# Two transformer blocks on one core: the down projections with products of 512 columns

## The chip, the cores and the metric

One core of a Trainium2 chip runs the whole program in one launch. The metric is device time in microseconds, from the first to the last instruction of the program, as the median of several runs.

## The reference

Two stacks of two layers each follow one another over 256 positions of width 1024, in float32. All four layers end in a feed-forward part with 2816 hidden units, and its last step is the down projection that this case is about:

```
first stack:   y = (silu(g) * v) @ w_out        (g, v: halves of a width-3 causal convolution of h @ w_in)
second stack:  y = (silu(x @ w_gate) * (x @ w_up)) @ w_down
both:          x = x + gate * rms_norm(y) * gain  (no gate in the second stack)
```

Ahead of the feed-forward parts stand a convolution mixer and differential attention (first stack), an RWKV-7 time mix and a gating unit with a spatial product (second stack). The first stack also takes shifts, scales and gates from `silu(c) @ mod_w`, a product of a vector with a 1024 x 12288 matrix, called the modulation below.

## The kernel before

Activations lie transposed: channels on the 128 partitions, the 256 positions along the free axis (`T = 256`), in 8 chunks of channels (`DC`) or 22 chunks of hidden units (`FC`). A float32 product is made of rounded operands: a weight tile is split into `hi` (rounded, by ScalarE, `weights_hi`, line 1370) and `lo = raw - hi` (by VectorE, `weights_lo`, line 1919), an operand into a high and a low part too, and the product is lo x high + hi x low + hi x high, three matmuls into one accumulating half bank (lines 740 to 742 in `layer` of the tensor block).

The weights come in units. A unit of a down projection holds 11 tiles of 128 x 128 (1408 columns, 704 KB); two units (even and odd) make one chunk of 128 outputs, over the 22 hidden chunks. So a down stage has 16 units, 8 pairs, and each pair sums 66 products in one bank (PS[0] or PS[2] in turn, columns 0 to 255). There are four such stages: ffn0_down, ffn1_down, glu0_down, glu1_down. Every other stage has units of 8 tiles (1024 columns). Units go through four slots of `raw`, `hi` and `lo`, and each engine goes through the units in order, in bodies of four units:

- SyncE issues the load of a unit's raw weights when `lo` of the unit four before is made, then the loads of the modulation rows that ride there.
- ScalarE, at unit u: rounds the weights of unit u + 2 (when TensorE is done with unit u - 2), then, at an odd unit, waits for TensorE's unit u and evacuates the bank (`with_square`): Square into `SQ` (line 1426), then Copy with a gain into `Y` (line 1427), which frees the bank.
- VectorE, at unit u: `lo` of unit u + 2, then the evacuation of its own, which the down stages don't have, then the riders: `mod_unit` (line 1925) multiplies 1024 modulation weights by the condition and sums them. ffn0_down has riders of 2, 1, 2 and 0 after the four units of every body; the other three down stages have none. After the last unit of ffn0_down, glu0_down and others the low parts of the next stage's first units are made in the same places.
- TensorE, at unit u: waits for `lo` of unit u and for the bank to be free, then makes the products.

The hidden units are split by GpSimd into `GH` and `GL` (line 2738 and 2740). Behind a down stage `out_layer` sums the squares over the channels with TensorE (line 757; GpSimd adds seven of the eight squares beforehand, line 2729), ScalarE takes the root, VectorE the inverse, TensorE spreads it (line 764), and VectorE's `residual` scales `Y` and adds it to `X` (lines 1978 and 1983). The next stage's operands follow from that. `keep_busy` (line 615) makes filler products with a constant tile.

Of the kernel before, what the change touches and what calls it, by code (L numbers as in the profile page):

```python
# [25 lines left out]
F32R = mybir.dt.float32r  # L26
ALU = mybir.AluOpType
ACT = mybir.ActivationFunctionType
AX_X = mybir.AxisListType.X
ds = bass.ds  # L30

P = 128
D = 1024
T = 256
# [162 lines left out]
def program(nc, w8, w11, wmod, par, con, xin, relb, crow, lora_in, lora_out, sgu_ws, sgu_bs, out):  # L197
    scratch = nc.dram_tensor("rel_bias_rows", (HEADS, 384), F32, kind="Internal").ap()

    with ExitStack() as ctx:  # L200
# [48 lines left out]
        def at(place, name, shape, dt=F32, plus=0):  # L249
            return nc.alloc_sbuf_tensor_at(name, shape, dt, offset=arena + (int(place * F) + plus) // 32 * 32)  # L250
# [6 lines left out]
        tmp = at(4, "tmp", [P, 4, 2, T])  # L257
        GH = at(5, "GH", [P, FC, T], F32R, plus=PHASE)
        GL = at(5, "GL", [P, FC, T], F32R, plus=PHASE + 4 * FC * T)
        modraw = at(5, "modraw", [P, SLOTS, D], plus=PHASE + 8 * FC * T)  # L260
# [350 lines left out]
        def _(pe):  # L611
# [99 lines left out]
            def layer(name, oh, ol, between=None, peel_first=False, fresh=False, after_chunk=None, beside=0, amid=None,  # L711
# [6 lines left out]
                def body(i, last):  # L718
                    both = together and isinstance(i, int) and i == 0
                    if both:  # L720
                        two_units(name, oh, ol, fresh, after_chunk, beside)
                        for r in range(2):
                            if between and start:
                                between(i, r)
                    for r in range(2 if both else 0, SLOTS):
                        u = start + 4 * i + r
                        k0 = kt * (r % 2) if down else 0
                        bank = PS[r - r % 2 if down else r]
                        pe.wait_ge(lo_made, u + 1)
                        if not (fresh and isinstance(i, int) and i == 0):  # L730
                            wait(pe, evac_done, u - 3)
                        elif r == 0:
                            pe.wait_ge(evac_done, start)
                        for k in range(kt):
                            if r == 0 or (down and r == 1):
                                pe.wait_ge(S("hidden_split") if down else operand_ready, ready_at[name] + k0 + k + 1)
                            w = slice(k * P, (k + 1) * P)
                            first = k == 0 and (not down or r % 2 == 0)
                            final = k == kt - 1 and (not down or r % 2 == 1)
                            pe.matmul(bank[:, 0:T], lo[:, r, w], oh[:, k0 + k], start=first, stop=False)  # L740
                            pe.matmul(bank[:, 0:T], hi[:, r, w], ol[:, k0 + k], start=False, stop=False)  # L741
                            ins = pe.matmul(bank[:, 0:T], hi[:, r, w], oh[:, k0 + k], start=False, stop=final)  # L742
                            if amid and k == kt // 2 - 1:
                                amid(i, r)
                            if after_chunk and isinstance(i, int) and i == 0 and r < 3:
                                after_chunk(r, k)
                            if beside and isinstance(i, int) and i == 0 and r == 0 and k < kt - 1:
                                keep_busy(1, 7, beside)
                        ins.then_inc(mm_done, 1)
                        if between:  # L750
                            between(i, r)
# [405 lines left out]
            def first_t(tb):  # L1157

                pe.wait_ge(S("tt_made"), 1)
                pe.wait_ge(S("level_by_act"), tb + 2)  # L1160
# [202 lines left out]
        def _(act):  # L1363
# [44 lines left out]
            def with_square(n, down, gain, biased=False):  # L1408
# [5 lines left out]
                def evacuate(i, r, u):  # L1414
# [3 lines left out]
                    c = 2 * i + r // 2 if down else 4 * i + r  # L1418
                    src = PS[r - 1 if down else r][:, 0:T]
                    if biased:  # L1420
# [369 lines left out]
            for tb in range(2):  # L1790
# [5 lines left out]
                               ).then_inc(S("level_by_act"), 1)  # L1796
            act.wait_ge(S("tt_made"), 1)
            for tb in range(2):
# [111 lines left out]
        def _(dve):  # L1910
# [292 lines left out]
            def conv_ffn_up(name, l):  # L2203
# [16 lines left out]
                layer(name, evacuate, made=1, peel_all=(name != LOOPED))  # L2220

            def glu_up(name, n):
                def evacuate(i, r, u):
# [18 lines left out]
            gate_gain(1, 3 * DC)  # L2242
            layer("ffn0_down", peel_all=True)
            residual(1, par_gain("kv_norm_g", 0))
# [119 lines left out]
            gate_gain(3, 7 * DC)  # L2364
            layer("ffn1_down")
            residual(3)
# [198 lines left out]
            def state_out(k):  # L2565
# [4 lines left out]
                for b in (g, g + 1):  # L2570
# [7 lines left out]
                          ).then_inc(S("tm_made"), 1)  # L2578
            dve.transpose(TTd[:].rearrange("p m t -> p t m"), U[:]).then_inc(S("tt_made"), 1)

# [19 lines left out]
            third_block(1)  # L2600
            dve.wait_ge(S("tt_made"), 1)
            dve.tensor_copy(TT[2 * BLK:3 * BLK, :, 2 * BLK:3 * BLK], TTd[2 * BLK:3 * BLK]).then_inc(S("level_by_dve"), 1)
# [58 lines left out]
            glu_up("glu0_up", 5)  # L2661
            layer("glu0_down", third=True)
            residual(5, par_gain("norm_g2", 4 * DC))
# [53 lines left out]
            glu_up("glu1_up", 7)  # L2717
            layer("glu1_down")
            residual(7)
# [3 lines left out]
        def _(pool):  # L2723
# [6 lines left out]

            flatH, flatL = (x[:].rearrange("p c t -> p (c t)") for x in (GH, GL))

# [131 lines left out]
```

## Time and profile before

| | |
|---|---|
| median of 3 runs | 1419.88 us (1414.57 to 1428.73) |
| the profiled execution, first to last instruction | 1420.2 us |
| granted TensorE clock, mean | 0.996 |
| TensorE busy | 1375.6 us, 97% |
| VectorE busy | 1049.1 us, 74% |
| ScalarE busy | 733.2 us, 52% |
| GpSimd busy | 219.2 us, 15% |

The profiled execution has no other time beside its span. PE is TensorE, PEld its weight loads, DVE is VectorE, ACT is ScalarE, POOL is GpSimd. Matmuls are pipelined and their ends are modelled: one lasts some 280 ns in the rows, while the next begins 113 to 118 ns after it, so their pace is read from starts. A granted clock of 1.00 is 2.4 GHz and one of 0.50 is 1.2 GHz. The four down stages lie at 283 to 345, 622 to 682, 1061 to 1122 and 1349 to 1409 us of the span.

### The profile page before, as it was taken

The numbers are of one execution on the slowest core, as the hardware profiler recorded it, in microseconds if no ns is written. First come the engines' busy times: TensorE is split into PE (matmuls) and PEld (weight loads), VectorE is DVE, ScalarE is ACT, GpSimd is POOL, SyncE is SP. The second block draws the span as 40 slices with busy tenths as digits, with TensorE's granted clock in tenths as the row PEclk, the third lists the DMA queues.
The fourth block names the chain that finished last, engine by engine and source line by source line (L and its number), as shares of the span: only waits on it lengthen the run. The fifth ranks groups of instructions, "written<-read, shape, count | busy, mean of one in ns | idle before, by whom it ended". The sixth has DMA issues, their size and how long they took to land.

```text
span 1420.2 us, 30753 instructions
## 1 busy us (share of the span) xinstructions
PE 1375.6 (97%) x11830; PEld 1310.7 (92%) x11830; DVE 1049.1 (74%) x1649; ACT 733.2 (52%) x1194; POOL 219.2 (15%) x232
## 2 busy tenths in 40 slices
PE   8999999999999999999999999999999999999997
PEld 6998899999988899999878888799999998999997
DVE  7988799987887889974787965777774556677743
ACT  4547555644556556664366442554444447544442
POOL 0000133310000223320000010113320000133300
PEclk9999999999999999999999999999999999999999
DMA  9874367797663547675322300346666433466661
GB/s 377 303 258 171 123 226 234 258 394 252 205 226 105 208 165 254 216 232 173 151 98 90 120 2 2 116 133 186 188 208 203 141 115 120 144 197 197 208 205 69
DMA packets 68434, 258.20 MB, mean 182 GB/s; under 512 B 7545, under 2 KB 9857, under 8 KB 67970
## 3 DMA queue, kind: packets, MB, share of 16 engines
q1 hardware_dynamic: 68354, 257.10, 54.2%
q8 instruction: 54, 0.88, 0.2%
q14 instruction: 26, 0.21, 0.0%
HBM read 256.01 MB, written 1.06 MB: 181 GB/s over the span
## 4 chain that ended last, share of the span: by engine, by line
PE 81%; DVE 11%; ACT 3%; issue 2%; DMA 2%; DVEq 0%; ACTq 0%
PE ps L740 21%; PE ps L742 20%; PE ps L741 20%; PE ps L757 3%; DVE lo L1919 2%; PE ps L701 2%; PE ps L703 1%; PE ps L702 1%; ACT hi L1370 1%; DMA modraw<-in_wmod 1%; DVE U L2508 1%; DMA modlast<-in_wmod 1%; DVE products L2506 1%; DVE modraw L1925 1%; PE ps L764 1%
## 5 line engine op out<-in xcount | busy, mean ns | idle before, releaser
L1919 DVE TENSOR_TENSOR lo<-raw,hi 128x1024 fp32r<-128x1024 f32 (+1 forms) x350 | 476.5, 1378 | 168.5 <-ACT hi L1370 167.8
L740 PE MATMUL ps<-OH,lo 128*128 128x256 f32 x1920 | 540.8, 282 | 6.2 <-DVE lo L1919 6.0
L742 PE MATMUL ps<-OH,hi 128*128 128x256 f32 x1920 | 534.8, 279 | 0.0
L741 PE MATMUL ps<-OL,hi 128*128 128x256 f32 x1920 | 534.8, 279 | 0.0
L1370 ACT ACTIVATE hi<-raw 128x1024 fp32r<-128x1024 f32 (+1 forms) x350 | 381.0, 1112 | 10.4 <-DMA raw<-in_w 6.1
L740 PEld LDWEIGHTS ps<-OH,lo 128*128 128x128 f32 x1920 | 362.0, 189 | 12.7 <-DVE lo L1919 9.9
L741 PEld LDWEIGHTS ps<-OL,hi 128*128 128x128 f32 x1920 | 362.4, 189 | 0.0
L742 PEld LDWEIGHTS ps<-OH,hi 128*128 128x128 f32 x1920 | 361.0, 188 | 0.0
L740 PE MATMUL ps<-GH,lo 128*128 128x256 f32 x704 | 196.3, 279 | 0.0
L742 PE MATMUL ps<-GH,hi 128*128 128x256 f32 x704 | 196.2, 279 | 0.0
L741 PE MATMUL ps<-GL,hi 128*128 128x256 f32 x704 | 196.2, 279 | 0.0
L2738 POOL CAST GH<-tmp 128x256 f32 x88 | 71.0, 807 | 515.5 <-DVE tmp L2201 515.5
L741 PEld LDWEIGHTS ps<-GL,hi 128*128 128x128 f32 x704 | 133.0, 189 | 0.0
L740 PEld LDWEIGHTS ps<-GH,lo 128*128 128x128 f32 x704 | 132.9, 189 | 0.1
L742 PEld LDWEIGHTS ps<-GH,hi 128*128 128x128 f32 x704 | 132.2, 188 | 0.0
L2729 POOL TENSOR_TENSOR SQ<-SQ 128x256 f32<-128x256 f32 x42 | 40.1, 955 | 494.3 <-ACT SQ L1426 494.0
L2740 POOL TENSOR_TENSOR GL<-tmp,GH 128x256 f32 x88 | 98.1, 1115 | 15.3 <-POOL GH L2738 15.3
L1492 ACT ACTIVATE tmp<-ps,par_sb 128x256 f32<-128x256 f32 x88 | 49.5, 565 | 92.8 <-PE ps L742 86.6
L1426 ACT ACTIVATE SQ<-ps 128x256 f32<-128x256 f32 (+1 forms) x56 | 21.5, 384 | 145.5 <-PE ps L742 144.1
L1925 DVE SCALAR_TENSOR_TENSOR modraw<-modraw,cond 128x1024 f32<-128x1024 f32 x71 | 87.0, 1239 | 7.0 <-ACT cond L1513 6.1
L1509 ACT ACTIVATE tmp<-tmp 128x256 f32<-128x256 f32 x44 | 18.4, 418 | 132.2 <-DVE tmp L2231 132.2
L701 PE MATMUL ps<-OH,lo 128*128 128x256 f32 x192 | 61.1, 318 | 10.0 <-DVE OL L2031 3.8
(389 smaller groups left out, 2059.5 us busy)
## 6 DMA issues: line engine op xcount, KB each, us to landing
raw<-in_w SPq DMA_DIRECT2D x288, 512.0 KB, 3.9
raw<-in_w SPq DMA_DIRECT2D x64, 704.0 KB, 5.3
modraw<-in_wmod SPq DMA_DIRECT2D x71, 512.0 KB, 5.2
modlate<-in_wmod SPq DMA_DIRECT2D x10, 512.0 KB, 4.0
modlast<-in_wmod SPq DMA_DIRECT2D x7, 512.0 KB, 4.5
modfirst_a<-in_wmod SPq DMA_DIRECT2D x4, 512.0 KB, 11.4
modfirst_b<-in_wmod SPq DMA_DIRECT2D x4, 512.0 KB, 12.1
l<-in_lora_in SPq DMA_DIRECT2D x1, 1536.0 KB, 6.2
```

The costliest lines, as they stand in the source:

```text
L701: pe.matmul(PS[r][:, 0:T], lo[:, r, w], oh[:, k], start=(k == 0), stop=False)
L740: pe.matmul(bank[:, 0:T], lo[:, r, w], oh[:, k0 + k], start=first, stop=False)
L741: pe.matmul(bank[:, 0:T], hi[:, r, w], ol[:, k0 + k], start=False, stop=False)
L742: ins = pe.matmul(bank[:, 0:T], hi[:, r, w], oh[:, k0 + k], start=False, stop=final)
L757: ins = pe.matmul(PS[4 + h][:, x * P:x * P + SAME], src[:, h * P:(h + 1) * P], ones[:, 0:SAME], start=first, stop=last)
L1370: act.activation(hi[:, s, 0:kt * P], raw[:, s, 0:kt * P], ACT.Copy).then_inc(hi_made, 1)
L1492: act.activation(tmp[:, kind, q], PS[r][:, 0:T], ACT.Identity, scale=flatpar[:, ds(w, 1)], bias=flatpar[:, ds(b, 1)]).then_inc(S("tap2_mad ...
L1919: dve.tensor_tensor(lo[:, s, 0:kt * P], raw[:, s, 0:kt * P], hi[:, s, 0:kt * P].bitcast(F32), ALU.subtract).then_inc(lo_made, 1)
L1925: stt(out=mod_at(m, s), in0=mod_at(m, s), scalar=1.0, in1=cond[:], op0=ALU.mult, op1=ALU.mult, accum_out=mod_sums[:, ds(m, 1)]).then_inc(m ...
L2729: pool.tensor_tensor(SQ[:, 0], SQ[:, 0], SQ[:, c], ALU.add).then_inc(S("sq_added"), 1)
L2738: pool.tensor_copy(flatH[:, ds(2 * T * i + q * T, T)], tmp[:, 3, q]).then_inc(S("hidden_hi"), 1)
L2740: pool.tensor_tensor(flatL[:, ds(2 * T * i + q * T, T)], tmp[:, 3, q], flatH[:, ds(2 * T * i + q * T, T)].bitcast(F32), ALU.subtract).then ...
```

## The change

`GH` and `GL` become the two halves of one tile `GB` at the same addresses. In the down stages the two products with `hi` become one: `hi` against both halves, 2 x 256 columns, into the whole bank. The product with `lo` still goes into the bank's first half. At every odd unit VectorE waits for TensorE and adds the two halves of the bank with a reduce into one of two slots of `xt` in SBUF; ScalarE waits for that and reads `xt` where it read the bank. Apart from that, two semaphores of the time mix become one (`tt_made` joins `tm_made`).

```diff
-        GH = at(5, "GH", [P, FC, T], F32R, plus=PHASE)
-        GL = at(5, "GL", [P, FC, T], F32R, plus=PHASE + 4 * FC * T)
+        GB = at(5, "GB", [P, 2, FC, T], F32R, plus=PHASE)
+        GH, GL = GB[:, 0], GB[:, 1]
...
                             final = k == kt - 1 and (not down or r % 2 == 1)
+                            if down:
+                                if first:
+                                    pe.matmul(bank[:, :], hi[:, r, w], GB[:, :, k0 + k], start=True, stop=False)
+                                    pe.matmul(bank[:, 0:T], lo[:, r, w], oh[:, k0 + k], start=False, stop=False)
+                                else:
+                                    pe.matmul(bank[:, 0:T], lo[:, r, w], oh[:, k0 + k], start=False, stop=False)
+                                    ins = pe.matmul(bank[:, :], hi[:, r, w], GB[:, :, k0 + k], start=False, stop=final)
+                                continue
                             pe.matmul(bank[:, 0:T], lo[:, r, w], oh[:, k0 + k], start=first, stop=False)
...
-                pe.wait_ge(S("tt_made"), 1)
+                pe.wait_ge(S("tm_made"), 2)
...
-                    src = PS[r - 1 if down else r][:, 0:T]
+                    if down:
+                        act.wait_ge(S("halves_added"), c + (DC * (n // 2) + 1))
+                    src = xt[:, 2 + r // 2] if down else PS[r][:, 0:T]
...
+            def add_halves(i, r, u):
+
+                if r % 2:
+                    dve.wait_ge(mm_done, u + 1)
+                    dve.tensor_reduce(xt[:, 2 + r // 2], PS[r - 1][:, :].rearrange("p (h t) -> p t h", h=2), AX_X, ALU.add
+                                      ).then_inc(S("halves_added"), 1)
...
-            layer("ffn0_down", peel_all=True)
+            layer("ffn0_down", add_halves, peel_all=True)
...
-            layer("ffn1_down")
+            layer("ffn1_down", add_halves)
...
-            layer("glu0_down", third=True)
+            layer("glu0_down", add_halves, third=True)
...
-            layer("glu1_down")
+            layer("glu1_down", add_halves)
```

`add_halves` is VectorE's evacuation: it stands behind the low part and ahead of the riders of its unit.

## Rows read from the trace of the kernel before

**Rows 1.** The page, busy time and share of the span by engine.

```profile
PE 1375.6 (97%) x11830; PEld 1310.7 (92%) x11830; DVE 1049.1 (74%) x1649; ACT 733.2 (52%) x1194; POOL 219.2 (15%) x232
```

**Rows 2.** The page, the chain that ended last, by line.

```profile
PE ps L740 21%; PE ps L742 20%; PE ps L741 20%; PE ps L757 3%; DVE lo L1919 2%; PE ps L701 2%; PE ps L703 1%; PE ps L702 1%; ACT hi L1370 1%; DMA modraw<-in_wmod 1%; DVE U L2508 1%; DMA modlast<-in_wmod 1%; DVE products L2506 1%; DVE modraw L1925 1%; PE ps L764 1%
```

**Rows 3.** Stages: window, us; busy (instructions) of PE, PEld, DVE, ACT, POOL; clock; DMA; GB/s.

```profile
282.60:345.00 62.40, 62.40 (x534) 62.32 (x533) 51.75 (x64) 27.30 (x34) 9.10 (x10) 1.00 0.91 348
618.60:680.50 61.90, 61.90 (x549) 61.90 (x548) 30.35 (x26) 29.18 (x36) 8.15 (x10) 1.00 0.57 185
...
1347.00:1409.00 62.00, 62.00 (x549) 62.00 (x548) 26.38 (x19) 25.53 (x31) 5.71 (x9) 1.00 0.42 143
```

**Rows 4.** Groups by line and form: busy us, mean ns, idle before.

```profile
L740 PE MATMUL ps<-GH,lo 128*128 128x256 f32 x704 | 196.3, 279 | 0.0
```

**Rows 5.** Timeline of ACT, three down stages: start, us, line, tiles, idle before.

```profile
290.51 0.38 ACT L1426 ACTIVATE SQ<-ps 128x256 f32 x1 [0.78 <-PE ps L742]
...
298.43 0.38 ACT L1426 ACTIVATE SQ<-ps 128x256 f32 x1 [3.60 <-PE ps L742]
...
306.20 0.39 ACT L1426 ACTIVATE SQ<-ps 128x256 f32 x1 [4.49 <-PE ps L742]
306.48 0.47 ACT L1427 ACTIVATE Y<-ps,rgain 128x256 f32 x1
306.84 1.38 ACT L1370 ACTIVATE hi<-raw 128x1408 fp32r<-128x1408 f32 x1
...
629.65 0.38 ACT L1426 ACTIVATE SQ<-ps 128x256 f32 x1 [1.95 <-PE ps L742]
...
637.12 0.39 ACT L1426 ACTIVATE SQ<-ps 128x256 f32 x1 [4.18 <-PE ps L742]
...
1114.67 0.38 ACT L1426 ACTIVATE SQ<-ps 128x256 f32<-128x256 f32 x1 [4.39 <-PE ps L742]
...
1118.62 1.06 ACT L1370 ACTIVATE hi<-raw 128x1024 fp32r<-128x1024 f32 x1 [1.30 <-PE ps L742]
1122.45 0.38 ACT L1426 ACTIVATE SQ<-ps 128x256 f32<-128x256 f32 x1 [2.77 <-PE ps L742]
```

**Rows 6.** Timeline of PE: products of 288 rounded columns, filler in unrounded float32.

```profile
48.73 0.30 PE L632 MATMUL ps<-dL,utH 128*128 128x288 f32 x1
...
49.27 0.29 PE L633 MATMUL ps<-dH,utH 128*128 128x288 f32 x1
...
694.19 2.11 PE L615 MATMUL ps<-con_sb 128*128 128x256 f32 x9
```

**Rows 7.** Groups by line and form: the reduces out of a bank.

```profile
L2309 DVE TENSOR_REDUCE small<-ps 128x2 f32<-128x512 f32 x8 | 5.5, 689 | 3.4 <-PE ps L892 3.4
...
L2309 DVE TENSOR_REDUCE small<-ps 128x2 f32<-128x256 f32 x8 | 3.3, 412 | 0.0
```

**Rows 8.** The chain that ended last, end of ffn0_down: start, us, what.

```profile
344.81 0.13 PE ps L742
...
344.97 0.39 ACT SQ L1426
...
345.40 0.70 PE ps L757 x4
```

**Rows 9.** Timeline of DVE, ffn0_down.

```profile
292.33 1.62 DVE L1919 TENSOR_TENSOR lo<-raw,hi 128x1408 fp32r<-128x1408 f32 x1
293.86 1.22 DVE L1925 SCALAR_TENSOR_TENSOR modraw<-modraw,cond 128x1024 f32<-128x1024 f32 x1
...
295.01 1.62 DVE L1919 TENSOR_TENSOR lo<-raw,hi 128x1408 fp32r<-128x1408 f32 x1
...
338.92 1.22 DVE L1919 TENSOR_TENSOR lo<-raw,hi 128x1024 fp32r<-128x1024 f32 x1 [0.76 <-ACT hi L1370]
```

**Rows 10.** Stages as in rows 3, around the first drop of the granted clock.

```profile
696.30:698.70 2.40, 0.33 (x3) 0.36 (x4) 2.37 (x6) 0.81 (x2) 0.00 (x0) 1.00 0.00 0
698.80:702.20 3.40, 3.40 (x18) 3.40 (x17) 3.33 (x9) 0.81 (x2) 0.00 (x0) 0.50 0.02 5
```

More of the change, by code:

```diff
@@ L1796, in _ @@
                                ).then_inc(S("level_by_act"), 1)
-            act.wait_ge(S("tt_made"), 1)
+            act.wait_ge(S("tm_made"), 2)
             for tb in range(2):
@@ L2578, in _ @@
                           ).then_inc(S("tm_made"), 1)
-            dve.transpose(TTd[:].rearrange("p m t -> p t m"), U[:]).then_inc(S("tt_made"), 1)
+            dve.transpose(TTd[:].rearrange("p m t -> p t m"), U[:]).then_inc(S("tm_made"), 1)
             def level_copy(to, bank, rows, width):
@@ L2600, in _ @@
             third_block(1)
-            dve.wait_ge(S("tt_made"), 1)
+            dve.wait_ge(S("tm_made"), 2)
             dve.tensor_copy(TT[2 * BLK:3 * BLK, :, 2 * BLK:3 * BLK], TTd[2 * BLK:3 * BLK]).then_inc(S("level_by_dve"), 1)
@@ L2729, in add_up @@
                     pool.tensor_tensor(SQ[:, 0], SQ[:, 0], SQ[:, c], ALU.add).then_inc(S("sq_added"), 1)
-            flatH, flatL = (x[:].rearrange("p c t -> p (c t)") for x in (GH, GL))
+            flatH, flatL = (x.rearrange("p c t -> p (c t)") for x in (GH, GL))
             def split_hidden(k):
```

## The prediction

> **What bounds the kernel now.** I read the busy line of the page first: TensorE is busy for 97% of the span and VectorE for 74% [rows 1]. The chain that ended last says whether that is the limit: 61% of it are the three products of line 740 to 742 [rows 2]. So a product saved is time saved, as long as nothing else becomes late. The four down stages then show what the average hides [rows 3]: TensorE is full in all four, but VectorE is busy for 51.75 of 62.40 us in ffn0_down and for 30.35 us of ffn1_down and 26.38 us of glu1_down (glu0_down lies between). The difference is the modulation: only ffn0_down carries riders (2, 1, 2 and 0 of them after the four units of a body).
>
> **The products.** Before, each of the 704 pairs of a weight tile and an operand chunk makes three products of 256 columns, so there are three groups like the one shown [rows 4]. After, it makes one of 256 and one of 512: as many columns, 704 weight loads and 704 instructions fewer. What is gained is only what a product costs beyond its columns. The pace before comes from ScalarE's Square, which runs once per pair of units, that is per 66 products: 306.20 - 298.43 = 7.77 us in ffn0_down and 1122.45 - 1114.67 = 7.78 us in glu0_down, but 637.12 - 629.65 = 7.47 us in ffn1_down, and glu1_down goes like it [rows 5]. So one product takes 0.118 us in two stages and 0.1133 us in the other two. Both paces occur in the same code at the same granted clock (1.00 [rows 3]), and each holds until the next stall; I assume that a stage keeps its pace.
>
> No rounded product of 512 columns stands in the trace. From below: nine filler products of unrounded float32 run back to back in 2.11 us [rows 6]. If the last one's record outlasts the next start as the 288-column records do (0.30 - 0.135 = 0.165 us), each takes (2.11 - 0.165) / 9 = 0.216 us, the longest streamed product that the trace has. From above: two products at the present pace, 0.2266 or 0.236. The widest rounded products, those of 288 columns, follow each other at (49.27 - 48.73) / 4 = 0.135 us [rows 6], so 0.017 us for 32 more columns against 0.118; by that slope, 512 would take 0.254, the far end. I take 0.220, between 0.216 and twice the better pace and nearer to the first, since a longer product leaves its successor's weight load more time to hide. At 0.1133 a pair then goes from 0.3400 to 0.3333 us, 6.7 ns x 176 = 1.2 us per stage; at 0.118 from 0.354 to 0.338, 16 ns x 176 = 2.8 us. For ffn1_down, glu0_down and glu1_down together that is 1.2 + 2.8 + 1.2 = 5.2 us less. ffn0_down is counted apart, below.
>
> The Trainium skill (TensorE: Matmul & The Clock Gate, section Back-to-back issue gap) gives an isolated gap of N / 2.4 + 2.5 ns, which is 216 ns for 512 columns and 109 ns for 256. The trace has 113 to 118 for 256, so the rule leaves out something here; with its 216 in place of 220 the three stages would gain another 2 us.
>
> **The adds at the end of a stage.** Each of the four stages makes eight sums on VectorE, 32 in all, each of 512 inputs to 256 outputs out of a bank. The nearest row is the same operation with as many inputs out of a bank, 0.689 us; with half as many it takes 0.412, my lower end [rows 7]. That the two halves lie 256 elements apart has no row; twice the first, 1.38 us, is my upper end. I take 0.69. In the middle of a stage the sum lies beside TensorE's next pair of units in the other bank (7.4 us for 0.69 and ScalarE's 0.7). Behind the last pair nothing covers it: the chain there goes from the last product to the Square, to the token sums, to the root [rows 8], and the sum with one hand-over of 0.03 us stands in front of the Square. That is 0.72 us in each of ffn1_down, glu0_down and glu1_down: 2.2 us more. ScalarE's Square and scaling read SBUF in place of a bank; I count that as nothing. The two semaphores made one, and the two tiles made one at the same addresses, cost nothing.
>
> **ffn0_down: a new ring.** Here the sum also adds a wait, and that is the largest term. VectorE works in order. At an odd unit it will make the low part that it makes now, then wait for the product and add, then do its rider. ScalarE, in order too, now waits for the sum, does Square and scaling, and only then rounds the next weight tile, which VectorE needs for its next low part. So one sum starts the chain that leads to the next sum. Its period, from rows of this stage: the sum 0.69, hand-over 0.03, Square 0.28 and scaling 0.36 to the next start, the rounding 1.38, hand-over 0.03 [rows 5]: 2.77 us until the low part can start (a rider of 1.15 fits into this time, and the rest of it VectorE idles); the low part 1.53 and two riders of 1.15, each to the next start, and the second low part 1.53 [rows 9]. Together 8.13 us, against 7.4 to 7.8 us in which TensorE does a pair. Behind this ring wait TensorE (for the low part) and, at the end, the residual.
>
> It also starts late. In the trace VectorE is free of the low part of unit 3 at 293.86, though the first bank is full at 290.4 (the Square of it starts at 290.51) [rows 5, 9]. The first sum thus starts at 293.86, 3.4 us late. Six periods follow, and a last one with tiles of 1024 columns (rounding 1.06, low parts 1.22 less 0.09 [rows 5, 9]): 2.45 + 1.13 + 2.30 + 1.13 = 7.01. The last sum starts at 293.86 + 6 x 8.13 + 7.01 = 349.7, and the last Square at 350.4, where it stands at 344.97 now [rows 8]: 5.4 us later. TensorE itself gets the low part of unit 4 at 293.86 + 2.77 + 1.62 = 298.2, that of unit 14 five periods later at 338.9, and ends two units (7.4 us) on, at 346.3: whatever its products gain in this stage is lost to waiting, and it then idles for 4 us.
>
> In the other three stages there are no riders, and the same ring takes 2.77 + 1.53 + 1.53 = 5.83 us, less than a pair's 7.3: no wait there.
>
> Twice in the trace the granted clock is 0.50, that is 1.2 GHz, for 3.4 us, and both times TensorE had been idle just before; the place shown is that near 700 us, with products in only 0.33 of 2.40 us before it [rows 10], the other lies near 1194. So I expect the same after the 4 us in ffn0_down. The work in these 3.4 us (token sums, spreading, filler, the first products of att_k) mostly waits for VectorE. Bounds: nothing, or half of 3.4 us; I take 0.9.
>
> **The sum**, against the profiled span of 1420.2 us (the median of the runs is 1419.88, so the profile stands for it): - 5.2 + 2.2 + 5.4 + 0.9 = + 3.3, so 1423.5 us, 0.2% slower. A measurement of this kernel tells about 1% from no change: the three runs spread from 1414.57 to 1428.73.
>
> **Rivals.**
> - The ring does not form: the sums fall into VectorE's 10.65 idle us of ffn0_down (eight need 5.5), and all four stages gain. 1420.2 - 5.2 - 2.8 + 4 x 0.72 = 1415.1. For it: the idle time is there. Against: it lies before low parts, waiting for ScalarE's rounding [rows 9], and the ring makes just that wait longer.
> - A strided sum out of a bank is dear. Each 0.1 us more counts eleven times (eight in the ring, three ends). At 1.38 us: 1431. From 1.65 us on the kernel is over 1% slower (1434.1). For it: no row has this stride. Against: both reduce forms of the trace go by the number of inputs (0.689 for 512, 0.412 for 256 [rows 7]).
> - 512 columns cost two products of the stage's pace: no gain, 1428.7. For it: the 288-column rows scale even more steeply than the columns. Against: the unrounded products show that a longer one closes the gap.
> - A 512-column product is far cheaper than its columns. At 0.131 us a pair of units would need 22 x (0.1133 + 0.131) = 5.4 us, the ring's 5.83 us would bind in the three stages, each would end 12 to 13 us sooner, and the time would be 1386. The 288-column row, already at 0.135, speaks against it. The same section of the Trainium skill states 131 ns for a sustained stream of N = 512 with its weight loads; no run here shows such a stream.
>
> **How the numbers follow.** Forecast 0.60, no ring 0.13, dear sum 0.12, no gain 0.12, cheap product 0.01, and 0.02 for what I don't see. Unknown prices around the forecast: the sum at 0.42 gives - 3.0 and at 1.38 + 7.6; the product at 0.216 gives - 2.1, at 0.236 + 8.4 and at 0.254 + 18; the clock - 0.9 to + 0.8. The pace that a stage falls into (0.0045 us per product, 4.8 us for an up stage of 1056) can differ from run to run by several us either way. From the low sides together and the run spread I take 1412, from the likelier high ones 1437. Over 1% faster (under 1406) holds only the cheap product and luck: 0.02. Over 1% slower takes the dearest sum, or the dear sum and no gain together: 0.08.
>
> **What would show it.** Right: 704 products of 512 columns, 0.21 to 0.23 us from start to start; a group of 32 sums near 0.69 us; in ffn0_down Squares 8.1 us apart, VectorE's low parts idle for ScalarE before the even units, the last Square about 4 us after the last product, and granted clock 0.5 soon after; in the other three stages Squares 7.3 to 7.5 us apart and a last Square 0.7 us after the last product. Wrong: sums much over 0.7 us, Squares in ffn0_down at 7.4 us, or a 512-column product that takes as long as two.

## The result, and the profile after

| | before | after |
|---|---|---|
| median, runs taken in turn | 1427.16 us (20 runs, 1414.55 to 1436.38) | 1435.12 us (20 runs, 1429.56 to 1440.78) |
| ratio of the times | | 1.0078, interval 1.0054 to 1.0101 |
| the profiled execution, its span | 1420.2 us | 1432.8 us |
| granted TensorE clock, mean | 0.996 | 0.993 |

By the ratio the change makes the kernel 0.8% slower; the two medians by themselves stand 8.0 us or 0.6% apart, which lies just inside the interval. The forecast was 0.2% slower, 1423.5 us; the sign and the mechanism in ffn0_down came as forecast, and one term was wrong in sign.

The page's busy time by engine, after [rows 1]:

```profile
PE 1382.7 (97%) x11126; PEld 1285.0 (90%) x11126; DVE 1071.0 (75%) x1681; ACT 735.1 (51%) x1194; POOL 216.4 (15%) x232
```

704 matmuls fewer, and TensorE is busy 7 us longer. VectorE's extra 22 us are the sums. The groups by line and form, after (busy us, mean ns, idle before); 32 more pairs of products stand under other lines of the same block [rows 4, 7]:

```profile
L746 PE MATMUL ps<-GB,hi 128*128 128x512 f32 x672 | 238.5, 397 | 0.0
L745 PE MATMUL ps<-GB,lo 128*128 128x256 f32 x672 | 188.7, 281 | 0.0
L2236 DVE TENSOR_REDUCE xt<-ps 128x256 f32<-128x512 f32 x32 | 22.0, 689 | 42.8 <-PE ps L746 42.8
```

The sum takes 0.689 us, the same as the reduce of as many inputs before [rows 7]. The stages after, with the columns of [rows 3]: ffn0_down, ffn1_down, glu1_down, and the second clock level behind ffn0_down:

```profile
282.90:345.30 62.40, 60.86 (x339) 51.85 (x338) 50.44 (x63) 25.70 (x32) 6.54 (x9) 1.00 0.89 333
628.80:691.20 62.40, 62.40 (x358) 54.27 (x356) 32.22 (x29) 27.69 (x33) 5.56 (x8) 1.00 0.53 172
1359.00:1421.00 62.00, 62.00 (x355) 53.95 (x354) 28.79 (x25) 25.33 (x30) 5.57 (x8) 1.00 0.43 140
353.50:357.00 3.50, 3.50 (x11) 2.93 (x12) 2.43 (x7) 2.86 (x5) 0.00 (x0) 0.51 1.04 345
```

ffn0_down is no longer full of products: TensorE is busy for 60.86 of 62.40 us in it. ffn1_down and glu1_down are full, but a full stage now takes longer. From the first product to the last, the four down stages took 62.0, 59.7, 62.1 and 59.7 us before and take 64.9, 61.8, 61.8 and 61.8 us after: the two that had the better pace have lost it. Where the time was lost along the program is read from the first scaling of each residual behind a down stage. VectorE's timeline, before and then after:

```profile
347.39 0.75 DVE L1978 TENSOR_TENSOR Y<-Y,ps 128x256 f32<-128x256 f32 x2 [0.80 <-PE ps L764]
...
684.40 1.28 DVE L1978 TENSOR_TENSOR Y<-Y,ps 128x512 f32<-128x512 f32 x2 [0.87 <-PE ps L764]
...
1124.87 0.75 DVE L1978 TENSOR_TENSOR Y<-Y,ps 128x256 f32<-128x256 f32 x2 [0.80 <-PE ps L764]
...
1412.05 1.28 DVE L1978 TENSOR_TENSOR Y<-Y,ps 128x512 f32<-128x512 f32 x2 [0.87 <-PE ps L764]
```

```profile
354.57 0.75 DVE L1988 TENSOR_TENSOR Y<-Y,ps 128x256 f32<-128x256 f32 x2 [1.21 <-PE ps L772]
...
694.51 1.29 DVE L1988 TENSOR_TENSOR Y<-Y,ps 128x512 f32<-128x512 f32 x2 [0.87 <-PE ps L772]
...
1134.38 0.75 DVE L1988 TENSOR_TENSOR Y<-Y,ps 128x256 f32<-128x256 f32 x2 [0.80 <-PE ps L772]
...
1424.66 1.28 DVE L1988 TENSOR_TENSOR Y<-Y,ps 128x512 f32<-128x512 f32 x2 [0.87 <-PE ps L772]
```

After is 7.2 us late behind ffn0_down, 10.1 behind ffn1_down, 9.5 behind glu0_down and 12.6 behind glu1_down. So the loss is in ffn0_down (7.2) and in ffn1_down and glu1_down (about 3 each); glu0_down costs 0.7. Between ffn1_down and glu0_down 1.3 us come back, 0.7 of them in the time mix, in this one execution.

**The ring in ffn0_down.** ScalarE's timeline after: two Squares and what stands between them, the last Square of the stage, and two Squares of ffn1_down [rows 5, 8]:

```profile
303.06 0.42 ACT L1436 ACTIVATE SQ<-xt 128x256 f32 x1 [4.95 <-DVE xt L2236]
303.39 0.49 ACT L1437 ACTIVATE Y<-xt,rgain 128x256 f32 x1
303.79 2.63 ACT L1378 ACTIVATE hi<-raw 128x1408 fp32r<-128x1408 f32 x2
...
311.38 0.42 ACT L1436 ACTIVATE SQ<-xt 128x256 f32 x1 [4.96 <-DVE xt L2236]
...
351.71 0.42 ACT L1436 ACTIVATE SQ<-xt 128x256 f32<-128x256 f32 x1 [4.43 <-DVE xt L2236]
...
637.71 0.42 ACT L1436 ACTIVATE SQ<-xt 128x256 f32 x1 [2.95 <-DVE xt L2236]
...
645.48 0.42 ACT L1436 ACTIVATE SQ<-xt 128x256 f32 x1 [4.40 <-DVE xt L2236]
```

The Squares in ffn0_down are 8.32 us apart (7.77 before), and each waits for the sum. In ffn1_down they are 7.77 apart (7.47 before); there TensorE is never idle, so that is the pace of the products. VectorE's timeline gives the start of the sum ahead of the first of these Squares:

```profile
302.25 0.68 DVE L2236 TENSOR_REDUCE xt<-ps 128x256 f32<-128x512 f32 x1
```

The chain that ended last shows what VectorE does in front of the last sum of ffn0_down:

```profile
346.37 1.23 DVE lo L1929
347.59 2.29 DVE modraw L1935 x4
349.88 1.14 DVE lo L1929
351.01 0.61 DVE xt L2236
...
351.71 0.43 ACT SQ L1436
...
690.93 0.24 PE ps L746
...
691.20 0.70 DVE xt L2236
...
691.99 0.43 ACT SQ L1436
```

At the end of ffn0_down the sum comes behind a low part, two riders and another low part; at the end of ffn1_down it comes straight behind the last product, and there the Square starts 1.06 us after the start of that product; before it was 0.16 [rows 8]. Of the 0.90 more the product is 0.11 longer (0.24 for 0.13), and the sum with its hand-overs is 0.8. TensorE's timeline after, behind ffn0_down:

```profile
347.79 0.39 PE L746 MATMUL ps<-GB,hi 128*128 128x512 f32 x1
...
352.18 0.69 PE L765 MATMUL ps<-con_sb,SQ 128*128 128x96 f32 x4 [3.57 <-ACT SQ L1436]
...
353.42 1.12 PE L772 MATMUL ps<-con_sb,tok 128*128 128x128 f32 x4
354.33 3.63 PE L615 MATMUL ps<-con_sb 128*128 128x256 f32 x10
```

The last Square is 3.9 us behind the start of the last product, TensorE idles for 3.57 us, and from 353.5 to 357.0 the granted clock is 0.51, near 1.2 GHz (windows above).

### The profile page after: what moved, and what is told of

Same layout as the page of the kernel before. It is cut to its first block, busy times and chain, and to the rows that moved or that the text cites. A ratio compares the mean times of both kernels' runs of the same rounds, so it can differ in the third digit from the quotient of the medians.

```text
span 1432.8 us, 29418 instructions
## 1 busy us (share of the span) xinstructions
PE 1382.7 (97%) x11126; PEld 1285.0 (90%) x11126; DVE 1071.0 (75%) x1681; ACT 735.1 (51%) x1194; POOL 216.4 (15%) x232
## 3 DMA queue, kind: packets, MB, share of 16 engines
HBM read 256.01 MB, written 1.06 MB: 179 GB/s over the span
## 4 chain that ended last, share of the span: by engine, by line
PE 78%; DVE 15%; ACT 4%; issue 2%; DMA 1%; ACTq 0%; DVEq 0%
PE ps L748 15%; PE ps L750 14%; PE ps L749 14%; PE ps L746 9%; PE ps L745 4%; DVE lo L1929 4%; PE ps L765 3%; DVE modraw L1935 2%; PE ps L701 2%; ACT hi L1378 2%; PE ps L702 1%; PE ps L703 1%; DMA modraw<-in_wmod 1%; PE ps L615 1%; DVE U L2525 1%
## 5 line engine op out<-in xcount | busy, mean ns | idle before, releaser
L746 PE MATMUL ps<-GB,hi 128*128 128x512 f32 x672 | 238.5, 397 | 0.0
L745 PE MATMUL ps<-GB,lo 128*128 128x256 f32 x672 | 188.7, 281 | 0.0
L746 PEld LDWEIGHTS ps<-GB,hi 128*128 128x128 f32 x672 | 126.3, 188 | 29.2
L2755 POOL CAST GB<-tmp 128x256 f32 x88 | 71.0, 807 | 513.9 <-DVE tmp L2211 513.9
L745 PEld LDWEIGHTS ps<-GB,lo 128*128 128x128 f32 x672 | 126.1, 188 | 1.5
L2757 POOL TENSOR_TENSOR GB<-tmp,GB 128x256 f32 x88 | 98.2, 1116 | 16.5 <-POOL GB L2755 16.5
L1436 ACT ACTIVATE SQ<-xt 128x256 f32 (+1 forms) x32 | 13.4, 418 | 143.5 <-DVE xt L2236 138.6
L615 PE MATMUL ps<-con_sb 128*128 128x256 f32 (+1 forms) x262 | 67.4, 395 | 2.3 <-ACT Btok L1786 1.2
L615 PEld LDWEIGHTS ps<-con_sb 128*128 128x128 f32 x262 | 49.9, 204 | 11.0 <-DMA con_sb<-in_con 2.0
```

Source lines behind the costliest of these rows:

```text
L615: pe.matmul(PS[bank][:, 0:width], ones, con_sb[:, 0:width], start=True, stop=True)
L745: pe.matmul(bank[:, 0:T], lo[:, r, w], oh[:, k0 + k], start=False, stop=False)
L746: ins = pe.matmul(bank[:, :], hi[:, r, w], GB[:, :, k0 + k], start=False, stop=final)
L2755: pool.tensor_copy(flatH[:, ds(2 * T * i + q * T, T)], tmp[:, 3, q]).then_inc(S("hidden_hi"), 1)
L2757: pool.tensor_tensor(flatL[:, ds(2 * T * i + q * T, T)], tmp[:, 3, q], flatH[:, ds(2 * T * i + q * T, T)].bitcast(F32), ALU.subtract).then ...
```

## The experiments

Two theories of the loss stood after this. The first: 512 rounded columns cost two products of the worse pace, in any surroundings, and the ring and the last sums cost the rest. The rival: the sums, the waits or the alternation of widths slow the products, and a 512-column product alone is cheaper. Beside it stood the question of the two paces.

### The product by itself

```diff
+            row(N, 0, lambda r, w, c: mm(T, hi[:, r, w], GB[:, 0, c]))
+            row(N, 0, lambda r, w, c: mm(2 * T, hi[:, r, w], GB[:, :, c]))
...
+            row(N, 0, lambda r, w, c: mm(2 * T, hi[:, 0, 0:P], flatG[:, T * c:T * (c + 2)]))
+            row(N, 0, lambda r, w, c: (mm(T, lo[:, r, w], GB[:, 0, c]), mm(2 * T, hi[:, r, w], GB[:, :, c])))
```

The kernel after, with rows of 96 products behind its last stage, so its own time says nothing. `row(N, ...)` issues what follows N times, and `mm` is a product of the given number of columns with a weight tile and an operand.

> The changed kernel with rows of products put behind its last stage, all into one bank, 96 each: 256 columns; 512 columns from the two halves of GB; 512, 384 and 128 columns in one run; 512 columns with one and the same weight tile; 256 (lo) and 512 (hi) in turn; 256 unrounded; 256 three at a time as before. Theory 1 (a rounded product costs by its columns): 0.235 us for 512 in every form (0.226 if the better pace shows), 0.176 for 384, 0.118 or 0.113 for 256, 0.353 for the pair. Rival (the operand's two runs, or the load of new weights, make it dear): two runs 0.235, one run or one weight tile near 0.216.

Windows inside the rows (columns of [rows 3]): 256 columns; 512 in two runs of 256; 512 in one run; 384; and, behind two rows left out, 256 and 512 in turn.

```profile
1426.00:1434.00 8.00, 8.00 (x70) 8.00 (x70) 3.40 (x6) 0.00 (x0) 0.00 (x0) 1.00 0.38 133
1437.00:1457.00 20.00, 20.00 (x87) 16.15 (x86) 0.00 (x0) 0.00 (x0) 0.00 (x0) 1.00 0.00 0
1459.00:1479.00 20.00, 20.00 (x88) 16.10 (x87) 0.00 (x0) 0.00 (x0) 0.00 (x0) 1.00 0.00 0
1481.00:1496.00 15.00, 15.00 (x88) 15.00 (x87) 0.00 (x0) 0.00 (x0) 0.00 (x0) 1.00 0.00 1
...
1532.00:1560.00 28.00, 28.00 (x160) 24.34 (x159) 0.00 (x0) 0.00 (x0) 0.00 (x0) 1.00 0.00 1
```

A window counts the products that overlap it, so the pace is the window and one record (0.40 for 512 columns), by the count: 20.40 / 87 = 0.234 and 20.40 / 88 = 0.232. The mean from start to start over the whole rows is 0.119 for 256 (0.118 once it streams), 0.233 for 512 (in one run or two), 0.234 with the weight tile kept, 0.175 for 384, 0.111 for 128, and 0.353 for a pair of 256 and 512. The last row, three products of 256 as in the kernel before, streams at 0.1133 in the same tail. Neither the split operand nor the weight load makes the 512 dear, as theory 1 had it: it takes 0.456 ns a column alone.

The row of 96 unrounded products of 256 columns left 192 records, 0.2158 us from start to start. So one such product leaves two records and takes 0.43 us. The kernel before shows the same: `keep_busy(1, 7)` is one filler product, and behind ffn0_down, at 345.93, it stands in the timeline as `128x256 f32 x2`. The row that the prediction leaned on thus counts halves of products, and it is no price of a product of 256 columns.

### Where the loss lies: the ring, the sums, the width

Each of the next five kernels takes one part of the change out. *The ring cut*: in ffn0_down ScalarE makes each evacuation one unit later, behind the rounding that it would hold up.

```diff
+                        elif r % 2 == 0 and 4 * i + r:
+                            evacuate(i - (r == 0), (r - 1) % SLOTS, start + 4 * i + r - 1)
...
+            layer("ffn0_down", with_square(1, True, own_gain(1)), peel_all=True, behind=True)
```

> The change, but in ffn0_down ScalarE rounds the next weight tile before it evacuates a pair, so that VectorE's next low part no longer waits for the sum. Theory 1 (the ring sum, Square, rounding, low part sets ffn0_down): Squares 7.8 us apart in place of 8.3, the last Square under 1 us after the last product in place of 3.7, no drop of the granted clock there, att_k about 6 us earlier, ratio to before about 1.004 in place of 1.008. Rival (VectorE has too much work there): still 8.3 us apart, ratio unchanged.

Measured: 1431.83 us (12 runs), ratio to before 1.0052 (1.0023 to 1.0081). ScalarE's timeline at the end of ffn0_down:

```profile
338.28 0.42 ACT L1441 ACTIVATE SQ<-xt 128x256 f32<-128x256 f32 x1 [3.55 <-DVE xt L2241]
...
346.03 0.42 ACT L1441 ACTIVATE SQ<-xt 128x256 f32<-128x256 f32 x1 [5.99 <-DVE xt L2241]
```

The Squares are 7.75 us apart, the residual starts at 348.49 where it was 354.57, and the clock stays at 1.00 behind the stage. That shows the ring: the same sums and products, in another order on ScalarE, and ffn0_down takes 61.9 us. In the medians the ratio falls only from 1.0078 to 1.0052, and the intervals overlap.

*The wide product split* into two of 256 columns in the two halves (the first of a bank stays whole):

```diff
-                                    ins = pe.matmul(bank[:, :], hi[:, r, w], GB[:, :, k0 + k], start=False, stop=final)
+                                    pe.matmul(bank[:, T:], hi[:, r, w], ol[:, k0 + k], start=False, stop=False)
+                                    ins = pe.matmul(bank[:, 0:T], hi[:, r, w], oh[:, k0 + k], start=False, stop=final)
```

> The change with its sums, but each product of 512 columns made as two of 256, one into each half of the bank (the first one of a bank stays whole). Theory 1 (columns cost the same either way, but narrow products can hold the better pace of 0.1133): ffn1_down and glu1_down last 59.8 us in place of 61.9, ffn0_down stays with its ring, ratio to before about 1.005. Rival (a wide product does save something): the down stages get longer than with the change, ratio above 1.008.

Measured: 1436.57 us (8 runs), ratio 1.0107 (1.0059 to 1.0155); down stages of 65.1, 62.1, 62.1 and 61.8 us, like the change's; the 59.8 of theory 1 did not come. So one product of 512 columns is worth just two of 256. But the pace stayed at the worse one in ffn1_down and glu0_down behind up stages that ran at the better, 0.1134; with one 512-column product left in each bank this said that something besides the width of every product sets the pace.

*No sums*: ScalarE reads the bank's first half as before; the product of `hi` with the operand's low part is thus left out of the output.

```diff
-                    src = xt[:, 2 + r // 2] if down else PS[r][:, 0:T]
+                    src = PS[r - 1 if down else r][:, 0:T]
...
-            layer("ffn0_down", add_halves, peel_all=True)
+            layer("ffn0_down", peel_all=True)
```

> The change's products without the sums: ScalarE reads the first half of the bank as before, so the product of hi and the operand's low part is left out of the result. Theory 1 (the wide product gains nothing and holds the worse pace): the four down stages last 61.9 us each, no ring, ratio to before 1.002 to 1.004. Rival (the loss is the sums' alone and the products gain): down stages of 58 to 60 us, ratio 0.995 to 0.998.

Measured: 1430.41 us (12 runs), ratio 1.0037 (1.0004 to 1.0070). Without ring and sums the down stages take 61.8 us each, as theory 1 had it, glu0_down behind an up stage at 0.1133: the wide products alone make the kernel slower, by 0.0037 x 1427 = 5.3 us (0.6 to 10 by the interval).

*Two banks, no wide product*: three products of 256 columns, the one with the low part into the neighbouring bank; the sum adds the two banks.

```diff
+                                pe.matmul(bank[:, 0:T], lo[:, r, w], oh[:, k0 + k], start=first, stop=False)
+                                pe.matmul(PS[r - r % 2 + 1][:, 0:T], hi[:, r, w], ol[:, k0 + k], start=first, stop=final)
+                                ins = pe.matmul(bank[:, 0:T], hi[:, r, w], oh[:, k0 + k], start=False, stop=final)
```

> The change with its sums, but without any product of 512 columns: hi times the operand's low part goes into the first half of the neighbouring bank, 256 columns like the other two, and VectorE adds the two banks' first halves. Theory P (products of unequal width push TensorE to the worse pace): each down stage keeps the pace of its up stage, so where the up stage runs at 0.1133 the down stage lasts 59.8 us. Rival Q (changing the place of the output from product to product does it, widths or not): 61.9 us and 0.118 in the down stages whatever the up stage does. Both: ffn0_down keeps the ring, last Square about 3.7 us after the last product.

Measured: 1430.57 us against 1420.95 (10 and 22 runs), ratio 1.0058 (1.0018 to 1.0099). ScalarE's timeline, two Squares of ffn1_down and two of glu0_down:

```profile
644.59 0.42 ACT L1433 ACTIVATE SQ<-xt 128x256 f32 x1 [4.12 <-DVE xt L2233]
652.07 0.42 ACT L1433 ACTIVATE SQ<-xt 128x256 f32 x1 [4.11 <-DVE xt L2233]
...
1095.15 0.42 ACT L1433 ACTIVATE SQ<-xt 128x256 f32 x1 [4.42 <-DVE xt L2233]
1102.92 0.42 ACT L1433 ACTIVATE SQ<-xt 128x256 f32 x1 [4.42 <-DVE xt L2233]
```

7.48 us apart in the one and 7.77 in the other: with products of one width each of the three stages without riders keeps the pace of its up stage, sums or no sums. ffn0_down still takes 65.1 us. So ring and sums cost 0.0058 x 1421 = 8.2 us without any wide product; with the 5.3 above that is 13.5 against the change's 0.0078 x 1427 = 11.1, inside the intervals.

*The change in all down stages but ffn0_down*:

```diff
-                            if down:
+                            if down and name != "ffn0_down":
```

> The change in ffn1_down, glu0_down and glu1_down, with ffn0_down as before. By the theory (ring 6 to 7 us in ffn0_down, 0.7 us for the last sum of each other stage, 61.9 us per stage in place of 59.8 where the better pace is lost): no gap behind ffn0_down, residual there at 347.5 us of the span as before, ratio to before 1.003 to 1.005. Rival (the loss is spread evenly over the four stages): three quarters of it, 1.006.

Measured: 1431.58 us (12 runs), ratio 1.0080 (1.0037 to 1.0123); stages of 62.2, 61.8, 61.8 and 61.8 us, residual behind ffn0_down at 348.63. The profile has the ring's 6 us back, the ratio does not; its interval is too wide to say how much of the ring's cost the medians hold.

### The two paces

*One wide product in front of each pair of units*, into a spare bank, in the kernel before:

```diff
+                            if down and first:
+                                pe.matmul(PS[7][:, :], hi[:, r, w], oh[:, 0:2], start=True, stop=True)
```

> The kernel before with one rounded product of 512 columns into a spare bank ahead of each pair of units of the down stages, its result unused. It costs 8 x 0.23 = 1.9 us per stage by itself. Theory P: the products after it run at 0.118 even where the up stage ran at 0.1133, so such a down stage lasts 62.0 + 1.9 us. Rival Q: they keep the up stage's pace, 59.8 + 1.9 us there.

Measured: 1435.40 us (4 runs), ratio 1.0119 (1.0045 to 1.0193). ScalarE's timeline in ffn1_down:

```profile
637.59 0.39 ACT L1428 ACTIVATE SQ<-ps 128x256 f32 x1 [4.42 <-PE ps L744]
...
645.59 0.39 ACT L1428 ACTIVATE SQ<-ps 128x256 f32 x1 [4.71 <-PE ps L744]
...
653.31 0.39 ACT L1428 ACTIVATE SQ<-ps 128x256 f32 x1 [4.43 <-PE ps L744]
```

8.00 and 7.72 us apart, and 8.00 again to the next: the products between two wide ones go at 0.1178 in one pair and at 0.1133 in the next. So a single wide product can change the pace of all that follow it up to the next, in both directions. Neither theory had that; all four down stages alternate so. The wide product itself takes 0.226 us behind products at 0.1133 and 0.231 behind products at 0.1178 (from its start to the next): beside the better pace it costs just two of 256, and the loss is in the products behind it.

*Extra products of other widths* in front of each pair: one of 256 columns in ffn1_down, two in glu0_down, one of 384 in glu1_down.

```diff
+                                for width in {"ffn1_down": (T,), "glu0_down": (T, T), "glu1_down": (3 * P,)}.get(name, ()):
+                                    pe.matmul(PS[7][:, 0:width], hi[:, r, w], oh[:, 0:2].rearrange("p c t -> p (c t)")[:, 0:width],
+                                              start=True, stop=True)
```

> The kernel before with extra rounded products into a spare bank ahead of each pair of units, results unused: one of 256 columns in ffn1_down, two of 256 in glu0_down, one of 384 in glu1_down. In the run with one of 512 the pace flipped at each of them between 0.1133 and 0.118. Theory W (a product of another width flips the pace): no flip in ffn1_down and glu0_down, a flip per pair in glu1_down, where the pairs alternate between 7.48 and 7.77 us. Theory N (an odd number of products flips it): a flip per pair in ffn1_down and in glu1_down, none in glu0_down.

One execution of 1450.21 us, in which all up stages ran at 0.118. The 256-column extras changed nothing: 0.1178 throughout. In glu1_down the Squares are 7.65 us apart, extra product included:

```profile
1399.27 0.39 ACT L1430 ACTIVATE SQ<-ps 128x256 f32 x1 [4.36 <-PE ps L746]
1406.92 0.39 ACT L1430 ACTIVATE SQ<-ps 128x256 f32 x1 [4.37 <-PE ps L746]
```

That is 0.1133 for the rest, from the first product of 384 on, and the next ones did not turn it back. Neither theory had that.

*One product of 512 columns in glu0_up*, behind its first four units, and one behind glu0_down:

```diff
+                    if isinstance(i, int) and i == 0 and r == SLOTS - 1 and name == "glu0_up":
+                        pe.matmul(PS[7][:, :], OH[:, 0, 0:P], OH[:, 0:2], start=True, stop=True)
...
+            pe.matmul(PS[7][:, :], GH[:, 0, 0:P], GH[:, 0:2], start=True, stop=True)
```

> The kernel before with two extra rounded products of 512 columns into a spare bank, results unused: one behind the first four units of glu0_up, one behind the last unit of glu0_down. In most profiles so far glu0_up runs at 0.118 and glu1_up at 0.1133. If one product of another width flips the pace until the next stall, the rest of glu0_up and glu0_down run at the better pace: 1037 and 528 products, 7 us less, ratio to before 0.995 to 0.998. If the pace is not carried that way, or is drawn anew in each execution, no change beyond the interval.

1415.13 us against 1420.02 (12 and 17 runs), ratio 0.9978 (0.9950 to 1.0006): no difference that the interval shows. In the profile glu0_up goes at 0.1178 up to the product and at 0.1133 behind it, and glu0_down with it (59.7 us); glu1_up, which has no such product, ran at 0.1178.

*One such product in each of the four up stages*, of 384 columns and, in a second kernel, of 512; its result is not used:

```diff
+                        if isinstance(i, int) and i == 0 and r == SLOTS - 1 and name in UP:
+                            pe.matmul(PS[7][:, 0:3 * P], oh[:, 0, 0:P], oh[:, 0:2].rearrange("p c t -> p (c t)")[:, 0:3 * P],
+                                      start=True, stop=True)
```

> The kernel before with one extra rounded product of 384 columns behind the first four units of each of the four up stages, into a spare bank, result unused. In the run with odd products glu1_down came out of its up stage at 0.118 and ran at 0.1133 from the first product of 384 on, and stayed there although seven more followed. Theory S (384 columns set the better pace, whatever it was): all four up stages and their down stages run at 0.1133 after it, median 1410 to 1414 us, ratio to before 0.990 to 0.996. Theory F (it flips, or does nothing reliable): some stages at 0.118 still, ratio 0.997 to 1.003.

> The same with products of 512 columns, which flipped the pace each time where one stood ahead of every pair. By theory F the four stages come out at either pace as chance has it before them, ratio to before 0.997 to 1.003; by a theory that any product of another width sets the better pace, all four at 0.1133 and ratio 0.990 to 0.996.

Measured with 384: 1416.20 us (9 runs), ratio 0.9931 (0.9894 to 0.9969). With 512: 1415.99 us (12 runs), ratio 0.9937 (0.9905 to 0.9969), before at 1427.45 (20 runs). Both are faster than the kernel before and, by the ratios to it, than the change. TensorE's timeline with 512, in glu0_up:

```profile
945.37 0.28 PE L742 MATMUL ps<-OH,hi 128*128 128x256 f32 x1
945.48 0.39 PE L753 MATMUL ps<-OH 128*128 128x512 f32 x1
945.71 0.28 PE L740 MATMUL ps<-OH,lo 128*128 128x256 f32 x1
```

Over some 20 products ahead of the wide one the mean from start to start is 0.1178 us, over the 24 behind it 0.1135. TensorE's windows in glu0_up and glu1_up (busy, count, clock, DMA share, GB/s), of the kernel before and then of the one with 512:

```profile
960.00:1050.00 90.00, 90.00 (x766) 1.00 0.62 188
1250.00:1340.00 90.00, 90.00 (x797) 1.00 0.64 195
```

```profile
960.00:1050.00 90.00, 90.00 (x797) 1.00 0.66 197
1250.00:1340.00 90.00, 90.00 (x797) 1.00 0.68 202
```

797 products in 90 us at the better pace, 766 at the worse. In the profiles of the kernels with such products in up stages (glu0_up alone, 384 and 512) the pace went from 0.1178 to 0.1133 at the product four times, and where it was 0.1133 already, five times, it stayed. In ffn0_up of the 512 kernel it fell back at 189 us, at a wait of a few hundredths of a microsecond, without any wide product near, came back at 204 and fell again at 226. In the 384 kernel it fell back at 189 too. So the ratios came as theory S had them, but not its condition that all four pairs of stages run at 0.1133: ffn0_up and ffn0_down ran mostly at 0.1178 in both. The span of the 512 kernel, 1413.1 us, is 7.1 below that of the kernel before, about as much as glu0_up and glu0_down gained.

## Why the prediction was right and wrong

**The products: the step that failed.** The term was - 5.2 us for three stages, from 0.220 for a product of 512 columns. It measured 0.235 beside a product of 0.118, and 0.233 alone. The stage lengths make the term + 2.1, - 0.2 and + 2.1, together + 4.0: that is 9.2 of the 9.3 us by which the span of 1432.8 missed 1423.5; the other misses, up and down, nearly cancel. Three choices were wrong. The lower end, 0.216, I read as an unrounded product of 256 columns [rows 6]; it is one of the two records of such a product, which takes 0.43, so it bounds nothing, and the argument that unrounded products show a longer one closing the gap falls with it. I let it pull the value away from the rounded products of 288 columns (0.135), though those have the operand type in question; by the column they give 0.469 ns, and 512 measured 0.456. And I assumed that a stage keeps its pace: with the widths mixed, every stage ran at the worse one, also behind up stages at 0.1134. The rival "512 columns cost two products of the stage's pace" was nearer, and still too mild for ffn1_down and glu1_down.

The isolated gap by the rule of the Trainium skill (TensorE: Matmul & The Clock Gate, section Back-to-back issue gap) is 216 ns for 512 columns. Rounded products of 512 columns took 226 to 236 here, so it is 4 to 9% short. The same section of the Trainium skill gives 131 ns for a sustained stream of N = 512, the cheap product among the rivals. The rows of 512 columns in the first experiment, at 0.232 to 0.234 us, do not agree with it, with new weights each time or with the tile kept.

**The sums: right.** 0.689 us measured, 0.69 taken; the distance of the halves costs nothing. At the end of ffn1_down the sum with its hand-overs puts the Square back by 0.8, where the term has 0.72; with the longer last product the end of each of the three stages costs 0.9.

**The ring: right in mechanism, its size a fifth short.** The period was worked out as 8.13 and measured 8.32; the last Square as 350.4 and came at 351.71, 6.7 us later than before instead of 5.4. The six periods make 1.0 of the missing 1.3 us, the first Square came 0.2 later than worked out, and the last, shorter period is 0.1 longer. Half of the 0.19 is what I counted as nothing: Square and scaling out of SBUF go 0.33 and 0.40 us to the next start, out of a bank 0.28 and 0.36 [rows 5], 0.09 together. The other half is the way from the sum to the Square, 303.06 - 302.25 = 0.81 from start to start where 0.72 was taken. There was no ring elsewhere, as forecast; moving the evacuation on ScalarE alone removes it.

**The clock: right in this execution.** Behind the ring's 3.57 idle us the clock was 0.51 for 3.5 us, and it was 0.50 there in the two other profiles with the ring (the wide product split, and two banks), behind 3.74 idle us. The last Square is 6.7 us late and the first product of att_k, at 357.61 where it was 349.95, 7.7: some 0.9 in between, the value taken. Not every pause does it. The kernel with the ring cut has the two later pauses of the kernel before too, 2.08 us near 700 [rows 10] and 3.02 near 1194, and its clock stayed at 1.00 behind both; and the changed kernel has one more stretch at 0.50, at 415 us, which the kernel before lacks.

**The sum again**, with the measured terms: the first product of ffn1_down is 7.1 us late (6.7 + 0.9, of which 0.5 come back), + 4.0 for the products and 3 x 0.9 for the ends make + 13.8, less the 1.3 ahead of glu0_down = 12.5, against 1432.8 - 1420.2 = 12.6 between the two spans. Whether those 1.3 us come from the two semaphores made one wasn't tried alone. They may be chance: with ffn0_down as before and the same code behind ffn1_down, the stretch from the last product of ffn1_down to the first of glu0_down took 381.1 us, here 378.1.

**The starting point.** The forecast took the profiled span of 1420.2 for the usual time, since the median of three runs was 1419.88. With 20 runs it became 1427.16: the profiled execution is one of the faster ones, and the 12.6 us between the profiles is more than the 8 to 11 us of the runs. So the account above is one of two executions, and only its parts that an experiment took out (the ring, the sums, the width) are shown beyond them. Among the rivals one price is off too: three stages that end 12 to 13 us sooner give 1390 to 1393, not 1386.

## What to carry to other kernels

Price a product from rows of its own operand type, and count how many records one product leaves before you read a price from them. Here the columns of rounded float32 cost about the same in wide products as in narrow ones, so merging two products saved nothing. A wait put on an in-order engine may close a ring (here sum, evacuation, rounding, low part) whose period is worked out from rows beforehand, and the cheapest cure is to move the waiting instruction behind the one that the ring needs. Read the pace of TensorE from start to start in each stage: a stage can run 4% slower than its twin at the same granted clock and full busy share.

## What the runs showed that I had not expected

The two paces of rounded products, 0.1133 and 0.1178 us for 256 columns at clock 1.00, are a state that persists over hundreds of products and, outside ffn0, passes from an up stage into its down stage. It differs between executions of the same stage, changes at short waits, and can change at a product of 384 or 512 columns, while extra ones of 256 left the worse pace as it was. One such product in each up stage made the kernel 0.6 to 0.7% faster. What sets the state stays open: the runs do not say why wide products in front of every pair turn it each time with 512 columns and not with 384, why one of 512 behind products at 0.1133 turned it there and not in the up stages, nor why mixed widths throughout stay at the worse pace. That the draw of this state makes the spread of the runs of before (mostly 1414 to 1437 us) is likely from the sizes, 0.0045 us x 1056 = 4.8 us in an up stage and 2.4 in a down stage. The recorded runs of before agree: they bunch near 1414, 1421, 1428 and 1435 us, some 7 us apart. It was not shown, since only one of those executions was profiled. If it holds, ratios of a few tenths of a percent here are in part this draw.
